# Two transformer blocks in one kernel: attention units weigh 2000 more in the sharing of expert rows beside the first half's block

## The chip, the cores and the metric

The kernel runs on one core of one Trainium2 chip. The metric is the device time of one execution in microseconds (us). Before the change the median of three runs is 4016.86 us (4007.53 to 4020.57).

## The reference, cut to what matters

512 tokens of width 1024, all in float32. A first block (RWKV and neighbourhood attention, not touched here) ends in a mixture of experts; a second block of two layers follows.

```python
# experts of the first block: 8 heads, 16 chosen rows of two tables per token and head
act = jax.nn.gelu(jnp.einsum('chkd,cd->chk', u_tab[i_c], x_c))
out = jnp.einsum('chk,chkd->cd', g_c * act, v_tab[i_c])

# second block, layer 0 (even mixer) and layer 1 (odd mixer: dilated attention)
for layer in range(2):
    x = x + mixers[layer](rms_norm(x, mix_norms[layer]))
    x = x + memory_cross_attention(rms_norm(x, xn), rms_norm(mem, mn), wq, wkv, wo)
    x = x + swiglu(rms_norm(x, fn), wg, wu, wd)      # hidden width 2816
return rms_norm(x, final_norm)
```

All attention of the second block is causal, so the first 256 tokens never need the last 256.

## The kernel before

The 512 tokens are four tiles of 128. Tiles 0 and 1 are the first half (h=0), tiles 2 and 3 the second half (h=1). For each tile, head and choice j (16 of them) POOL gathers two rows per token out of the tables by an indirect DMA (L2353, 128 rows of 4 KB, 0.52 MB): a u row, of which DVE takes the dot product with the token (`peer_dve`, L2483: a custom instruction and a read of its accumulator), and a v row, which DVE multiplies by the gated factor and adds to the tile's sum (L2469; for the first tiles TensorE does most of that). After the 16 dots of a head ACT takes their gelu (L2451) and DVE multiplies by the gates (L2491). The ring of buffers for gathered rows holds 8 of them in this phase.

While tiles 2 and 3 go through their experts (2 tiles x 8 heads x 16 choices = 256 steps, here called **slots**: one v row added, one u dot taken; the last 16 slots have a v row only), the whole second block for the first half of the tokens, called the block, is computed beside them: `second_pe`, `second_act` and `second_dve` with h=0. Afterwards the same code runs for h=1 with nothing beside it.

The three programs are generators that yield a number, a cost in made-up units, after each piece of work. `Beside` (L2357) shares them out: with the sum of all costs divided by 256, each slot lets the block go on until the costs it passed have used up the slot's part. DVE's program calls it twice a slot, once after the v row and once after the u dot. So the costs decide where in DVE's one instruction queue the rows of the experts stand between the instructions of the block:

```python
block = Beside(second(k, p, 0), k.second_cost, 16 * KN)     # L2391
...
def advance(self, part=1.0):                                 # L2363
    self.owed += self.each * part
    while self.owed > 0:
        x = next(self.steps, None)
        ...
        self.owed -= x
```

The block's stages are, in order: the experts' result and norms, `inputs_*` (7 products), 32 attention **units** of layer 0 (`units_pe`, `units_act`, `units_dve`; 16 of the sliding window, 16 latent), the output product, the cross attention's product and 8 units, its output product, the feed-forward (`ffn_*`, eleven rounds of gate, up and down products, each with 1 MB of weights), and the same again for layer 1 with 32 dilated units. The weights of each product come through four buffers of 1 MB (`load_wide`, L2780) and each is issued on SP's queue when the product before it in its buffer has ended. TensorE's products all stand in one helper (L2806, and L3684 for down).

A unit is one tile and one head: TensorE's scores (L3121), DVE's minimum with the mask (L3230, or L3234 for the cross attention), ACT's exp (L3191 or L3195), TensorE's transposes (L3153), ACT's copy (L3203), TensorE's output (L3162), DVE's division (L3252, L3257), and for every second one a transpose and a copy into the output (L3168, L3206). `unit_order` (L3053) pipelines them: while unit u is scored, unit u-1 is put out. Beside the units of layer 0 and of the dilated attention stand pieces of further products (`Fill`), one or two of which are taken per unit. Each unit ends in `yield unit_cost(x)`, where x.m is its number of keys (128 or 256 for h=0); the pieces of a product yield 427 for each of its matmul steps (`MM`).

Of the kernel before, what the change touches and what calls it, by code (L numbers as in the profile page):

```python
# [3094 lines left out]


def unit_cost(unit):
    return unit.m * 5 + 300


def both_halves(units, u):
# [25 lines left out]
def units_pe(k, p, a, name, units, fill, rate):  # L3127
    S, filled, made = k.S, 0, set()
    for step, u in unit_order(units):
# [6 lines left out]
        elif step == "rest":  # L3136
            yield from fill.rest()
        elif step == "pause":
            yield unit_cost(x)
        elif step == "scores":  # L3140
            yield from fill.until(x.mark, u - 1)
# [29 lines left out]
def units_act(k, p, a, name, units, fill, rate):  # L3171
    S = k.S
    for step, u in unit_order(units):
# [3 lines left out]
        if step == "fill":  # L3177
            yield from fill.take(rate, min(u + 1, len(units) - 1))
        elif step == "rest":
            yield from fill.rest()  # L3180
        elif step == "pause":
            yield unit_cost(x)
        elif step == "scores":
            yield from fill.until(x.mark, u - 1)
            s, bank = a.S[u % 2], k.bank[2 + u % 2]
            if x.nb < x.m and u >= 2:
                p.wait_ge(S.weights_filled, (name, u - 2))
            p.wait_ge(S.scores_low, key)
            if x.nb:
                last = x.nb == x.m and x.sink is None  # L3190
                p.e.activation(s[:, 0:x.nb], s[:, 0:x.nb], ACT.Exp, bias=low, scale=-1.0, accum_out=cols[:, 2:3]).then_inc(  # L3191
                    *(p.up(S.weights_exp, key) if last else p.up(S.scalar_step)))
            if x.nb < x.m:
                c = 3 if x.nb else 2
                p.e.activation(s[:, x.nb:x.m], bank[:, x.nb:x.m], ACT.Exp, bias=low, scale=-1.0,  # L3195
                               accum_out=cols[:, c:c + 1]).then_inc(*p.up(S.weights_exp, key))
            if x.sink is not None:
                p.e.activation(cols[:, 3:4], x.sink, ACT.Exp, bias=low, scale=-1.0).then_inc(*p.up(S.weights_exp, key))
        elif step == "weights" and weights_by(k, a, u) is S.act_weights:
            if u >= 2:  # L3200
                p.wait_ge(S.output_filled, (name, u - 2))
            p.wait_ge(S.weights_filled, key)
            p.e.activation(a.PT[u % 2][:, 0:x.m], k.bank[4][:, 0:x.m], ACT.Copy).then_inc(*p.up(S.act_weights, key))  # L3203
        elif step == "store" and stored_by(k, a, x.tile) is S.act_stored:
            p.wait_ge(S.store_filled, key)
            p.e.activation(x.dst, k.bank[4][:, 0:P], ACT.Copy).then_inc(*p.up(S.act_stored, key))  # L3206


def units_dve(k, p, a, name, units, fill, rate):
    S, stored = k.S, {}  # L3210
    for step, u in unit_order(units):
# [5 lines left out]
        elif step == "rest":  # L3217
            yield from fill.rest()
        elif step == "pause":
            yield unit_cost(x)  # L3220
        elif step == "scores":
            yield from fill.until(x.mark, u - 1)
# [935 lines left out]
```

## Time and profile before

| | |
|---|---|
| median of three runs | 4016.86 us (4007.53 to 4020.57) |
| profiled execution, its own time | 4020.22 us |
| its span, first to last instruction | 4018.4 us |
| TensorE busy | 3351.1 us (83%) |
| VectorE busy | 2197.6 us (55%) |
| ScalarE busy | 745.1 us (19%) |
| GpSimd busy | 1385.0 us (34%) |
| bytes moved | 834.04 MB |

The profile is of one execution. Busy shares are averages over stages with different limits, so they have to be read by stretches of the span. The phase in which the block stands beside the experts of tiles 2 and 3 goes from about 1815 to 2976 us.

### The profile page before, as it was taken

The page shows a single profiled execution, that of the slowest core. Times are in us where ns is not written, and L with a number is a line of the kernel's source. Part 1 is how long each engine was busy: PE and PEld are TensorE (multiplying, and loading weights), DVE is VectorE, ACT ScalarE, POOL GpSimd, SP SyncE. Part 2 cuts the span into 40 slices and gives each one's busy share as a digit, 9 for nine tenths or more (in the row PEclk, how much of TensorE's full clock was granted, in tenths as well). Part 3 has the DMA queues.
Part 4 walks back from the last instruction along what each step waited for, and adds up shares of the span by engine and source line. Part 5 has one row for each costly group of instructions (what it writes and reads, how often), then busy time and mean ns, then how long its engine had stood idle before and what let it go on. Part 6 is the DMA issues. An engine that isn't in the chain of part 4 may idle for free. (4 is left out here: it accounts for less than half of the span.)

```text
span 4018.4 us, 40100 instructions
## 1 busy us (share of the span) xinstructions
PE 3351.1 (83%) x14758; PEld 2479.8 (62%) x14758; DVE 2197.6 (55%) x4302; ACT 745.1 (19%) x1691; POOL 1385.0 (34%) x1219
## 2 busy tenths in 40 slices
PE   7778998888777787756677888778998999999999
PEld 3445647887333343424466776567876678877787
DVE  2434135455899989877677668877753320033201
ACT  2122122221211111111222002211012220022200
POOL 0641002221677767765344655545610000000000
PEclk9888889999888898988788999889999999999999
DMA  7230200003999999997578999879962134421343
GB/s 208 72 115 11 81 27 1 1 13 101 344 334 379 360 365 368 374 357 288 202 259 296 392 394 368 290 257 383 392 214 68 53 105 147 157 95 63 115 147 105
DMA packets 449223, 834.04 MB, mean 208 GB/s; under 512 B 46659, under 2 KB 291454, under 8 KB 449022
## 3 DMA queue, kind: packets, MB, share of 16 engines
q0 software_dynamic: 147456, 536.94, 35.9%
q1 hardware_dynamic: 301574, 294.56, 22.9%
q8 instruction: 118, 1.93, 0.2%
q14 instruction: 75, 0.61, 0.0%
HBM read 829.23 MB, written 2.17 MB: 207 GB/s over the span
## 5 line engine op out<-in xcount | busy, mean ns | idle before, releaser
L2806 PE MATMUL banks<-arena 128*128 128x256 f32 (+1 forms) x4992 | 1138.5, 387 | 80.5 <-DMA arena<-in_l_w_up 36.8
L2806 PEld LDWEIGHTS banks<-arena 128*128 128x128 f32 (+1 forms) x4992 | 961.8, 194 | 243.1 <-DMA arena<-in_l_w_up 40.8
L2353 POOL DMA_INDIRECT arena<-in_peer_u,arena x512 | 580.9, 1135 | 493.6 <-DVE arena L2483 185.1
L2353 POOL DMA_INDIRECT arena<-in_peer_v,arena x512 | 586.5, 1145 | 405.4 <-DVE arena L2469 244.4
L2483 DVE CUSTOM_DVE_ANT_0 arena<-arena 128x1024 f32<-128x1024 f32 x512 | 628.1, 1227 | 104.1 <-DMA arena<-in_peer_u,arena 80.0
L2425 PE MATMUL banks<-arena 128*128 128x512 f32 x768 | 415.6, 685 | 194.6 <-issue 68.4
L2469 DVE SCALAR_TENSOR_TENSOR arena<-arena 128x1024 f32<-128x1024 f32 x316 | 406.2, 1286 | 29.2 <-DMA arena<-in_peer_v,arena 15.1
L2425 PEld LDWEIGHTS banks<-arena 128*128 128x128 f32 x768 | 158.2, 218 | 408.4 <-issue 319.1
L3730 DVE TENSOR_TENSOR arena<-banks,arena 128x512 f32<-128x512 f32 x44 | 30.5, 692 | 514.9 <-PE banks L2806 514.8
L3684 PE MATMUL banks<-arena 128*128 128x256 f32 x1408 | 310.5, 378 | 0.0
L3684 PEld LDWEIGHTS banks<-arena 128*128 128x128 f32 x1408 | 265.7, 189 | 38.3
L842 PE MATMUL banks<-arena 128*128 128x512 f32 (+1 forms) x320 | 133.5, 567 | 39.0 <-DVE arena L986 18.2
L3705 ACT ACTIVATE arena<-banks 128x512 f32<-128x512 f32 x44 | 26.3, 598 | 687.0 <-PE banks L2806 629.8
L547 PE MATMUL banks<-arena 128*128 128x512 f32 (+1 forms) x336 | 131.4, 551 | 0.0
L1633 POOL TENSOR_TENSOR arena<-arena 128x512 f32<-128x512 f32 x48 | 52.5, 1093 | 222.3 <-DVE arena L1599 149.1
L2138 PE MATMUL banks<-arena 128*128 128x512 f32 (+1 forms) x320 | 123.5, 533 | 6.2 <-ACT arena L1911 3.5
L3230 DVE CUSTOM_DVE_ANT_0 arena<-banks,arena 128x256 f32<-128x256 f32 (+3 forms) x128 | 59.8, 467 | 122.5 <-PE banks L3121 115.7
L842 PEld LDWEIGHTS banks<-arena 128*128 128x128 f32 x320 | 65.5, 215 | 94.8 <-issue 68.6
L509 POOL TENSOR_TENSOR arena<-arena 128x2048 f32<-128x2048 f32 x16 | 57.3, 3603 | 193.1 <-ACTq L277 104.8
L3191 ACT ACTIVATE arena<-arena 128x256 f32<-128x256 f32 (+3 forms) x128 | 69.4, 542 | 293.1 <-DVE arena L3230 217.5
L3162 PE MATMUL banks<-arena 128*128 128x64 f32 (+1 forms) x720 | 119.0, 300 | 3.0 <-DVE arena L3257 3.0
L3153 PE MATMUL banks<-arena 128*128 128x128 f32 x360 | 80.4, 319 | 48.7 <-ACT arena L3206 32.8
(339 smaller groups left out, 4141.2 us busy)
## 6 DMA issues: line engine op xcount, KB each, us to landing
arena<-in_l_w_gate SPq DMA_DIRECT2D x44, 1024.0 KB
arena<-in_l_w_up SPq DMA_DIRECT2D x44, 1024.0 KB
arena<-in_l_w_down SPq DMA_DIRECT2D x44, 1024.0 KB
arena<-in_ada_w SPq DMA_DIRECT2D x24, 1024.0 KB, 8.6
arena<-in_l_w_qkv SPq DMA_DIRECT2D x24, 1024.0 KB
arena<-in_w_in SPq DMA_DIRECT2D x33, 512.0 KB
arena<-in_l_w_out SPq DMA_DIRECT2D x16, 1024.0 KB
arena<-in_peer_q_w SPq DMA_DIRECT2D x20, 512.0 KB
```

Of the source, the lines that this page charges most:

```text
L547: ins = p.e.matmul(k.bank[b][0:m, 0:n], k.W[slot][:, c, 0:m], rhs(c), start=c == 0, stop=c == c_n - 1, skip_group_check=True)
L842: ins = p.e.matmul(k.bank[b][0:m, 0:n], k.W[slot][:, c, 0:m], rhs(c), start=c == 0, stop=c == c_n - 1, skip_group_check=True)
L2138: ins = p.e.matmul(k.bank[4][:, cols], ws[j][:, c, :], k.HT[:, c, cols], start=c == 0, stop=c == DC - 1, skip_group_check=True)
L2353: p.e.indirect_dma_start(e.ring[slot], None, tables[table], bass.IndirectOffsetOnAxis(ap=e.IDX[h][:, t, j:j + 1], axis=0)).then_inc(*p.up( ...
L2425: ins = p.e.matmul(k.bank[b], e.diag[x % 4], e.ring[slot][:, half * T:half * T + T], start=h == 0 and j == 0, stop=h == HEADS - 1 and j == ...
L2469: p.e.scalar_tensor_tensor(out=e.ACC[t], in0=e.ring[slot], scalar=factor, in1=e.ACC[t], op0=ALU.mult, op1=ALU.add).then_inc(*p.up(S.rows_a ...
L2483: p.e.tensor_tensor_reduce(out=e.prod, in0=e.ring[slot], in1=e.H2[:, t, :], scale=1.0, scalar=0.0, op0=ALU.mult, op1=ALU.add, accum_out=e. ...
L2806: ins = p.e.matmul(out, left(c), right(c), start=c == 0, stop=c == c_n - 1, skip_group_check=True)
L3153: ins = p.e.transpose(k.bank[4][:, j * P:j * P + P], a.S[u % 2][:, j * P:j * P + P], k.ident)
L3162: ins = p.e.matmul(k.bank[5][:, 0:x.w], a.PT[u % 2][:, j * P:j * P + P], values, start=j == 0, stop=j == len(x.values) - 1, skip_group_che ...
L3191: p.e.activation(s[:, 0:x.nb], s[:, 0:x.nb], ACT.Exp, bias=low, scale=-1.0, accum_out=cols[:, 2:3]).then_inc(*(p.up(S.weights_exp, key) if ...
L3684: ins = p.e.matmul(k.bank[4 + o // 2][:, o % 2 * TH:o % 2 * TH + TH], w[:, r, P * o:P * o + P], a.hid[:, (i - 1) % 2, TH * r:TH * r + TH], ...
```

## The change

`unit_cost` returns 2000 more. Nothing else is edited:

```diff
 def unit_cost(unit):
-    return unit.m * 5 + 300
+    return unit.m * 5 + 2300
```

With h=0 there are 80 units, so the sum of the block's costs goes from 871,824 to 1,031,824 and the part of one of the 256 slots from 3405.6 to 4030.6. The costs that the code yields, added up by stage and divided by that part, give the slots that stand beside each stage:

| stage of the block, h=0 | units | cost before | slots before | slots after | difference |
|---|---|---|---|---|---|
| experts' result and 7 norms and scalings | 0 | 43,156 | 12.7 | 10.7 | -2.0 |
| inputs, 7 products | 0 | 47,234 | 13.9 | 11.7 | -2.2 |
| units of layer 0, while products stand beside them | 25 | 57,654 | 16.9 | 26.7 | +9.8 |
| units of layer 0, the last ones alone | 7 | 9,140 | 2.7 | 5.7 | +3.1 |
| products into and out of the cross attention, output products | 0 | 109,312 | 32.1 | 27.1 | -5.0 |
| cross units, two groups of 8 | 16 | 25,280 | 7.4 | 14.2 | +6.8 |
| feed-forward, two of 11 rounds | 0 | 450,912 | 132.4 | 111.9 | -20.5 |
| dilated units, while products stand beside them | 20 | 114,016 | 33.5 | 38.2 | +4.7 |
| dilated units, the last ones alone | 12 | 15,120 | 4.4 | 9.7 | +5.3 |

The instructions of TensorE, GpSimd and SP's queue keep their order. On VectorE rows change places with the block's instructions; on ScalarE the gelus do.

VectorE, among the last dilated units, before:

```order
L3257 TENSOR_SCALAR arena<-banks,arena 128x64
L2469 SCALAR_TENSOR_TENSOR arena<-arena 128x1024
L3230 ISA arena<-banks,arena 128x128
L3230 ISA arena 128x1
L3252 RECIPROCAL arena<-arena 128x1
L3257 TENSOR_SCALAR arena<-banks,arena 128x64
L3230 ISA arena<-banks,arena 128x256
L3230 ISA arena 128x1
L3252 RECIPROCAL arena<-arena 128x1
L3257 TENSOR_SCALAR arena<-banks,arena 128x64
```

The same place now:

```order
L3257 TENSOR_SCALAR arena<-banks,arena 128x64
L2483 ISA arena<-arena 128x1024
L2483 ISA arena 128x1
L2469 SCALAR_TENSOR_TENSOR arena<-arena 128x1024
L3230 ISA arena<-banks,arena 128x128
L3230 ISA arena 128x1
L3252 RECIPROCAL arena<-arena 128x1
L3257 TENSOR_SCALAR arena<-banks,arena 128x64
L2483 ISA arena<-arena 128x1024
L2483 ISA arena 128x1
L2469 SCALAR_TENSOR_TENSOR arena<-arena 128x1024
L3230 ISA arena<-banks,arena 128x256
```

Where one v row stood in two units, a u dot and a v row now stand in each.

VectorE in the feed-forward of layer 0, the start of one piece of the difference (L3730 closes a round of gate and up):

```order
+L2483 ISA arena<-arena 128x1024
+L2483 ISA arena 128x1
+L2469 SCALAR_TENSOR_TENSOR arena<-arena 128x1024
 L3730 TENSOR_TENSOR arena<-banks,arena 128x512
-L2469 SCALAR_TENSOR_TENSOR arena<-arena 128x1024
-L2483 ISA arena<-arena 128x1024
-L2483 ISA arena 128x1
-L2469 SCALAR_TENSOR_TENSOR arena<-arena 128x1024
```

Between two L3730 there are six slots in most rounds before and five in most rounds now.

ScalarE among the cross units of layer 0, one piece of the difference:

```order
 L3206 ACTIVATE arena<-banks 128x128
 L3203 ACTIVATE arena<-banks 128x256
+L2451 ACT_TABLE_LOAD
+L2451 ACTIVATE arena<-arena 128x16
+L3195 ACT_TABLE_LOAD
 L3195 ACTIVATE arena<-banks,arena 128x256
 L3206 ACTIVATE arena<-banks 128x128
```

A gelu with a table load before it and one behind it now stands between two units there.

## Rows read from the trace of the kernel before

**Rows 1.** The page: span, busy time of the engines, DMA share in 40 slices.

```profile
span 4018.4 us, 40100 instructions
PE 3351.1 (83%) x14758; PEld 2479.8 (62%) x14758; DVE 2197.6 (55%) x4302; ACT 745.1 (19%) x1691; POOL 1385.0 (34%) x1219
DMA  7230200003999999997578999879962134421343
```

**Rows 2.** Busy time by stretch: the two feed-forwards of the block.

```profile
core 0: us, PE busy (x) PEld busy (x) DVE busy (x) ACT busy (x) POOL busy (x), PEclk, DMA share, GB/s
2167.30:2429.60 262.30, 234.44 (x1041) 201.10 (x1042) 180.98 (x225) 17.72 (x23) 157.92 (x133) 0.97 1.02 386
2730.30:2975.90 245.60, 221.63 (x992) 190.13 (x991) 151.01 (x178) 17.72 (x23) 126.33 (x109) 0.97 0.98 366
```

**Rows 3.** Waits of PE and DVE, 2167.3 to 2429.6 us: total, times, longest.

```profile
PE banks L2806 <- DMA arena<-in_l_w_up: 18.8, 5, 5.1
PE banks L2806 <- DMA arena<-in_l_w_gate: 7.2, 3, 3.5
...
DVE arena L3730 <- PE banks L2806: 51.3, 11, 11.1
```

**Rows 4.** DMA in the same stretch: packets, MB, share of 16 engines.

```profile
DMA packets 43246, 101.21 MB, mean 386 GB/s; under 512 B 2575, under 2 KB 23899, under 8 KB 43233
...
q0 software_dynamic: 18582, 67.67, 66.4%
q1 hardware_dynamic: 24651, 33.37, 35.5%
```

**Rows 5.** By stretch: ten rounds, first to last L3730, twice with rows, once without.

```profile
2185.00:2419.80 234.80, 208.86 (x932) 178.94 (x931) 154.84 (x188) 15.62 (x20) 142.21 (x119) 0.97 1.04 394
2742.00:2973.90 231.90, 207.93 (x929) 178.17 (x928) 138.81 (x163) 15.62 (x20) 117.51 (x102) 0.97 0.99 370
3297.20:3498.10 200.90, 200.90 (x930) 175.38 (x929) 6.92 (x10) 5.98 (x10) 0.00 (x0) 1.00 0.47 152
```

**Rows 6.** By stretch: layer 0 units with products, alone; dilated units with products, alone.

```profile
1914.60:2036.00 121.40, 80.73 (x316) 52.76 (x314) 83.31 (x212) 39.49 (x128) 38.94 (x36) 0.76 0.60 200
2036.00:2051.60 15.60, 8.39 (x31) 6.26 (x30) 9.61 (x28) 4.65 (x18) 4.17 (x4) 0.61 0.67 212
...
2449.10:2589.00 139.90, 114.92 (x546) 91.43 (x544) 120.67 (x220) 35.20 (x100) 84.16 (x69) 0.95 0.96 346
2589.00:2615.10 26.10, 17.83 (x68) 12.74 (x69) 17.53 (x49) 7.92 (x30) 6.97 (x8) 0.50 0.53 157
```

**Rows 7.** By stretch: eight cross units for h=1 without rows, twice for h=0.

```profile
3240.20:3267.70 27.50, 18.73 (x104) 14.16 (x103) 10.18 (x32) 8.62 (x26) 0.00 (x0) 0.88 0.06 19
2110.30:2142.50 32.20, 17.52 (x69) 12.23 (x67) 17.54 (x36) 10.19 (x33) 8.04 (x10) 0.62 0.60 208
2669.40:2701.80 32.40, 17.46 (x69) 11.93 (x67) 17.57 (x36) 10.21 (x33) 7.88 (x9) 0.63 0.59 205
```

**Rows 8.** DVE's instructions in order: start, us; one slot with nothing between.

```profile
2298.24 1.28 DVE L2469 SCALAR_TENSOR_TENSOR arena<-arena 128x1024 f32<-128x1024 f32 x1
2299.55 1.23 DVE L2483 CUSTOM_DVE_ANT_0 arena<-arena 128x1024 f32<-128x1024 f32 x1
2300.71 0.08 DVE L2483 DVE_READ_ACCUMULATOR2_ANT arena<- 128x1 f32 x1
2300.82 1.28 DVE L2469 SCALAR_TENSOR_TENSOR arena<-arena 128x1024 f32<-128x1024 f32 x1
```

**Rows 9.** Gelus on ACT and the wait for them on DVE, 1815 to 2980 us.

```profile
L2451 ACT ACT_TABLE_LOAD  x15: 1283/1283/1283, 1901.2 to 2916.0; - x15
...
DVE arena L2491 <- ACT arena L2451: 17.2, 12, 8.3
```

**Rows 10.** By stretch: inputs; output product of layer 0; a norm and scaling.

```profile
1868.40:1914.60 46.20, 42.79 (x207) 36.34 (x206) 42.24 (x54) 5.50 (x10) 32.03 (x27) 1.00 0.93 346
2051.60:2080.20 28.60, 26.43 (x113) 22.71 (x114) 23.84 (x33) 2.54 (x8) 17.89 (x15) 0.86 0.83 287
2429.60:2449.10 19.50, 12.08 (x37) 9.14 (x36) 14.45 (x23) 5.79 (x8) 4.71 (x5) 0.65 1.00 367
```

## The prediction

> **What bounds the kernel now.** I read the page first, then the table of stretches, then the waits and the DMA view inside single stretches. The page [rows 1] says only that TensorE leads with 83% and that DMA is nearly full in the middle of the span, where the block stands beside the experts. The change acts in that phase alone, about 1815 to 2976 us, so the rest keeps its time.
>
> By stretch the phase falls into two kinds. In the feed-forwards the 16 DMA engines are full: share 1.02 and 0.98, at 386 and 366 GB/s [rows 2]. TensorE there waits for the weights of up and gate, 18.8 and 7.2 us in the first one, and DVE, which has little else to do, waits 51.3 us for TensorE [rows 3]. Two thirds of the DMA share are gathered rows, 67.7 MB of 101.2 [rows 4]. What this costs is read by comparing ten rounds beside rows with ten rounds of the same products in the second half with none beside them: 234.8 and 231.9 us against 200.9 [rows 5]. So the rows make the two feed-forwards about 34 and 31 us longer.
>
> In the units the reader sees the opposite. With the DMA share at 0.5 to 0.6 (0.96 only where the dilated products stand beside them), the limit is DVE's queue and the short chain TensorE, DVE, ACT, TensorE. DVE is busy 69% of the time in the units of layer 0, 86% in the dilated ones with products, 67% in the last dilated ones [rows 6] and 54% in the cross units [rows 7].
>
> **The change, part by part.** The cost table tells where slots go; the prices come from rows. One slot on DVE is 2.58 us: v row to v row, 2298.24 to 2300.82 [rows 8].
>
> 1. Feed-forwards, 10.3 slots fewer in each (66.2 to 55.9). In the first one the gathered 67.7 MB become 67.7 x 55.9 / 66.2 = 57.1, with 33.4 MB of weights 90.5 MB; at 386 GB/s that takes 234.6 us instead of 262.3, a gain of 27.7 [rows 2, 4]. TensorE's own floor is 262.3 - 33.9 = 228.4 [rows 2, 5]. DMA would still bind, by 6 us; two limits that close do not overlap perfectly, and I take 24. The second loses as many slots, its last 16 gather only one row each, and its cap is 31.0 [rows 5]; I take 23. Sum **-47**, bounds -36 and -65 (both caps reached).
>
> In the Trainium skill, the page "DMA: Bandwidth & Descriptors", section "Specifications", gives about 358 GB/s as the limit of HBM for one core. The 386 GB/s of [rows 2] lie above that, so here the measurement decides; by 358 the first feed-forward's gain would be an estimated 30 us and not 27.7.
>
> 2. Seven norms and scalings, inputs, output and cross products: 2.0, 2.2 and 5.0 slots fewer. In a norm's stretch DVE is busy 14.5 of 19.5 us and TensorE only 12.1, so DVE and its chain set the time [rows 10]: 2.0 x 2.58 = 5.2, taken as -5. In the inputs TensorE is busy 42.8 of 46.2 us, in the output product 26.4 of 28.6 [rows 10]: there a slot was nearly free, and taking it away gives -2 together. Sum **-7**, bounds 0 and -12.
>
> 3. Units of layer 0 with products, 9.8 slots more: DVE's 83.3 us busy become 83.3 + 9.8 x 2.58 = 108.6. As the slot's 2.6 us of DVE work fit into the time that the chain of the unit takes on ACT and TensorE, I expect waits to shrink until DVE is as full as in the dilated units with products, 120.7 / 139.9 = 86% [rows 6]: 108.6 / 0.863 = 125.8 against 121.4, **+4**. The last seven: (9.6 + 3.1 x 2.58) / 0.863 = 20.4 against 15.6, **+5**.
>
> 4. Dilated units with products, 4.7 slots more, where DVE and DMA are both full already: each slot at its full price, **+12**. The last twelve: (17.5 + 5.3 x 2.58) / 0.863 = 36.1 against 26.1, **+10**.
>
> 5. Cross units, 3.4 slots more in each group: (17.5 + 8.8) / 0.863 = 30.5, under the present 32.3, so they would hide. But the 3.7 slots now there cost 32.3 - 27.5 = 4.8 us, 1.3 each [rows 7]. Between 0 and 1.3 x 3.4 = 4.4 I take +1 each, **+2**.
>
> 6. ScalarE's gelus. Four of them (after slots 16, 64, 176 and 192) go from input, norm or feed-forward stretches to units, the others stay in their kind of stretch. Between exps each needs two table loads of 1.28 us, and DVE waits for them, now 17.2 us over 12 waits [rows 9]; among the units these loads stand in the chain. **+4** for the four less what their old places cost, bounds 0 and +8.
>
> TensorE's, POOL's and SP's orders are unchanged, so nothing is queued behind a new wait there. POOL waits for DVE to free ring buffers; a row that comes later on DVE is gathered later, and in the units the DMA share of 0.6 leaves room for it.
>
> The sum: -47 - 7 + 4 + 5 + 12 + 10 + 2 + 4 = **-17 us**, against the profiled execution's 4020.2 us: 4003. That execution is 3.4 us above the median of 4016.9, so in terms of the median the sum gives 4000; I say **4001**. Bounds: every moved slot absorbed in layer 0 and cross units (+0, with +22 for the dilated ones) and the caps reached give -65 - 12 + 22 = -55; all 29.7 slots at full price (+77) with the gelus at +8 and the small gains give -36 + 77 + 8 = +49.
>
> **The rivals.** A difference within 0.3%, 12 us, can't be told from no change for this kernel.
>
> *Absorbed.* The units of layer 0 and the cross units take their slots into waits wholly, and the feed-forwards come down to TensorE's floor: -60 - 7 + 22 + 4 = -41, so 3976. For it: DVE idles 38 us in the layer 0 units with products [rows 6] and only 25 us of work come. Against: the 1.3 us per slot in the cross units, where DVE is just as idle.
>
> *DVE saturated, the other side: slower.* A row is 1.2 to 1.3 us long and not divisible, and DVE takes its queue in order. If the v rows and u dots stand just before the minimum or the division that TensorE and ACT wait for, each moved slot costs its full 2.58 us, and the unit stages grow by 29.7 x 2.58 = 77. Against this the gains stay: -47 - 7 + 77 + 4 = +27, 4044. It decides from a mean of 1.7 us per moved slot (50 us of net gains over 29.7). For it: the last dilated units are a dense chain, and the dilated stage has no DVE time left. Against: 1.3 us in the only place where a price can be read [rows 7].
> A worsening goes with it. The granted clock is 0.95 in the dilated units with products, but 0.76 in those of layer 0, which have more gaps, and 0.50 in the last ones [rows 6]. If sparser products bring the dilated stage to 0.76, TensorE's 114.9 us become 114.9 x 0.95 / 0.76 = 144, above the stage's 139.9, and some 8 us come on top: 4052. The Trainium skill's "TensorE: Matmul & The Clock Gate", section "What's actually happening", states that the throttled clock is the default and activity releases it; by that rule thinner product stretches lose clock, and the rows at 0.76 and 0.50 agree with it.
>
> *Break-even.* The feed-forward gains are real but the units give them back at 1.3 to 2 us a slot: between -10 and +10, 4008 to 4028. That the change does nothing of what it says is excluded, as the order on DVE shows it.
>
> **How the numbers follow.** Forecast, between -30 and -5 us: 0.42. Absorbed or better, beyond -30: 0.13. Break-even, -5 to +10: 0.21. Saturated, above +10: 0.24, of which 0.05 with the lost clock. Over 12 us faster needs the sum at -12 or beyond: all of "absorbed" and 0.31 of the forecast, 0.44 together. Slower by over 12 us: 0.22 of the saturated case. The rest, 0.34, lies within. The range from **3974 to 4040** leaves out about one in ten on each side; it reaches to "absorbed" below and nearly to the saturated value above. Cases of both signs hold much of the chance; the likeliest one's own range is 3987 to 4012.
>
> **What would show it.** Right, step by step: ten rounds of feed-forward between first and last L3730 take 212 to 216 us, with TensorE's waits for up and gate under 10 us in the first (26.0 now); units of layer 0 take about 9 us longer in all, the dilated units about 22, cross groups stay within 2 us of 32; DVE's busy share in the units of layer 0 is near 86%; the second half's 1042 us from 2976 to the end do not move. Wrong: ten rounds over 225 us, which would mean DMA or the rows' order binds in another way; or unit stages longer by over 60 us in sum, with TensorE waiting for L3257 and L3230; or a granted clock near 0.8 in the dilated units with products.

## The result and the profile after

The changed kernel takes 4027.22 us (median of 19 runs, 4011.53 to 4037.50), the kernel before 4012.85 us (median of 19, 4000.91 to 4031.13). The ratio is 1.0032, with a 95% interval of 1.0020 to 1.0044: slower by about 13 us. I had forecast 4001 us, faster by 16; the measured time lies in the range, but on the other side of no change. The two profiled executions are no fair pair in their totals: that of before was 7 us above its median, that of after (4014.18 us) 13 us below. The parts of the span outside the changed phase differ by as much as the change does: behind the last L3730 of the first half come 1044.5 us before and 1030.5 after, and the eleven kernels of the experiments lie between these two whatever their weight. So I go by stages.

The busy time by stretch of the changed kernel, between the marks that answer to [rows 5], [rows 7] and [rows 6]: layer 0 units from first minimum to last division, cross units, ten rounds, dilated units, cross units, ten rounds.

```profile
core 0: us, PE busy (x) PEld busy (x) DVE busy (x) ACT busy (x) POOL busy (x), PEclk, DMA share, GB/s
1909.90:2077.90 168.00, 95.31 (x335) 62.36 (x335) 127.85 (x285) 46.19 (x149) 82.08 (x64) 0.65 0.71 236
2132.20:2171.40 39.20, 17.98 (x69) 12.68 (x67) 25.32 (x46) 12.96 (x36) 18.15 (x13) 0.60 0.64 213
2210.70:2418.60 207.90, 203.96 (x930) 176.23 (x929) 130.93 (x161) 14.32 (x19) 112.00 (x99) 0.99 1.04 392
2467.80:2642.50 174.70, 117.21 (x510) 90.21 (x508) 144.28 (x275) 40.84 (x128) 106.00 (x84) 0.79 0.91 316
2696.00:2735.00 39.00, 17.77 (x69) 12.50 (x67) 25.32 (x46) 12.93 (x36) 17.24 (x13) 0.60 0.63 212
2776.60:2981.90 205.30, 202.09 (x930) 174.94 (x929) 116.08 (x137) 14.32 (x19) 91.05 (x81) 1.00 0.97 364
```

And the same marks of the kernel before for the two unit stages that [rows 6] had cut in two (times in the texts and tables are taken from the exact starts and ends, so they can differ by 0.1 us from these rounded windows):

```profile
1919.00:2056.60 137.60, 87.83 (x335) 58.51 (x335) 94.98 (x245) 44.63 (x147) 41.56 (x39) 0.73 0.59 193
...
2472.10:2615.00 142.90, 109.73 (x509) 85.06 (x508) 116.41 (x241) 40.03 (x126) 75.52 (x63) 0.86 0.89 315
```

Side by side, in us, with the rest of the phase (norms, inputs, cross and output products and the ends of the feed-forwards) in one line. The slots of the cost table belong to whole stages; the column "counted" has the rows (L2469 and L2483) that the two traces show between these marks, two rows to a slot:

| stage | slots by cost | counted | before | after | difference | forecast |
|---|---|---|---|---|---|---|
| layer 0 units | +12.9 | +13 | 137.7 | 168.0 | +30.3 | +9 |
| cross units, both groups | +6.8 | +6 | 64.6 | 78.1 | +13.5 | +2 |
| dilated units | +10.0 | +11 | 142.9 | 174.7 | +31.8 | +22 |
| ten rounds of feed-forward, twice | -20.5 (eleven rounds) | -18.5 | 466.7 | 413.1 | -53.6 | -47 |
| the rest | -9.2 | -11.5 | 330.9 | 321.0 | -9.9 | -7 |
| all | 0 | 0 | | | +12.1 | -17 (with +4 for gelus) |

The waits in the first feed-forward show its limit gone: TensorE's waits for up and gate fall from 26.0 us [rows 3] to 3.9, and ten rounds stand 7 us from the 200.9 us without rows [rows 5].

```profile
PE banks L2806 <- DMA arena<-in_l_w_up: 3.4, 2, 2.5
PE banks L2806 <- DMA arena<-in_l_w_gate: 0.5, 1, 0.5
```

The units took the gain and more: 75.6 us for 30 counted slots, 2.5 us a slot on average, nearly VectorE's own 2.58 us of [rows 8]. The cross units tell why a stage in which VectorE is busy only 65% of the time hides nothing. One period of the changed kernel, in order of time (each `...` stands for lines left out):

```profile
2142.40 0.35 DVE L3257 TENSOR_SCALAR arena<-banks,arena 128x128 f32<-128x128 f32 x1 [2.27 <-PE banks L3162]
2142.78 1.23 DVE L2483 CUSTOM_DVE_ANT_0 arena<-arena 128x1024 f32<-128x1024 f32 x1
2142.93 0.42 PE L3168 MATMUL banks<-arena 128*128 128x128 f32 x1
...
2144.05 1.28 DVE L2469 SCALAR_TENSOR_TENSOR arena<-arena 128x1024 f32<-128x1024 f32 x1
...
2145.37 0.42 DVE L3234 TENSOR_REDUCE arena<-banks 128x1 f32<-128x256 f32 x1
2145.83 0.47 ACT L3195 ACTIVATE arena<-banks,arena 128x256 f32<-128x256 f32 x1 [3.91 <-DVE arena L3234]
...
2146.29 0.27 ACT L3206 ACTIVATE arena<-banks 128x128 f32<-128x128 f32 x1
...
2146.70 0.66 PE L3153 MATMUL banks<-arena 128*128 128x128 f32 x2 [3.35 <-ACT arena L3206]
2147.16 1.06 PE L3162 MATMUL banks<-arena 128*128 128x128 f32 x4
...
2148.36 0.35 DVE L3257 TENSOR_SCALAR arena<-banks,arena 128x128 f32<-128x128 f32 x1 [2.30 <-PE banks L3162]
```

It is a ring, a closed chain of waits (not the ring of buffers). The rows stand between a division and the next minimum. The minimum releases the exp; ScalarE's queue holds the copy L3206 of the block stored before behind that exp, though L3168, whose result it copies, had ended at 2143.35, nearly 3 us earlier; TensorE's transposes L3153 write into the bank that this copy reads, the output follows them, and the next division waits for the output. TensorE's waits of L3153 for that copy in this group (2132.2 to 2171.4 us) are

```profile
PE banks L3153 <- ACT arena L3206: 16.8, 6, 4.3
```

From division to division it takes 5.96 us, 2.97 of them from the one division to the next minimum, with a u dot and a v row in series. With one row there the trace of before has 4.70 us:

```profile
2123.19 0.35 DVE L3257 TENSOR_SCALAR arena<-banks,arena 128x128 f32<-128x128 f32 x1 [2.30 <-PE banks L3162]
2123.57 1.29 DVE L2469 SCALAR_TENSOR_TENSOR arena<-arena 128x1024 f32<-128x1024 f32 x1
...
2124.89 0.42 DVE L3234 TENSOR_REDUCE arena<-banks 128x1 f32<-128x256 f32 x1
...
2127.89 0.35 DVE L3257 TENSOR_SCALAR arena<-banks,arena 128x128 f32<-128x128 f32 x1 [2.30 <-PE banks L3162]
```

So the second row in a period costs 1.26 us, its whole length. Idle time of an engine inside such a ring is not room.

### The profile page after: what moved, and what is told of

It reads as the page before. It is cut to its first block and busy times, and to the rows that moved or that the text cites. A ratio compares the mean times of both kernels' runs of the same rounds, so it can differ in the third digit from the quotient of the medians.

```text
span 4012.4 us, 40100 instructions
## 1 busy us (share of the span) xinstructions
PE 3327.4 (83%) x14758; PEld 2464.1 (61%) x14758; DVE 2199.0 (55%) x4302; ACT 743.8 (19%) x1691; POOL 1393.6 (35%) x1219
## 3 DMA queue, kind: packets, MB, share of 16 engines
q0 software_dynamic: 147456, 536.94, 36.1%
## 5 line engine op out<-in xcount | busy, mean ns | idle before, releaser
L2483 DVE CUSTOM_DVE_ANT_0 arena<-arena 128x1024 f32<-128x1024 f32 x512 | 628.0, 1227 | 92.1 <-DMA arena<-in_peer_u,arena 73.0
L2425 PE MATMUL banks<-arena 128*128 128x512 f32 x768 | 406.0, 669 | 201.7 <-ACT arena L2444 131.4
L2469 DVE SCALAR_TENSOR_TENSOR arena<-arena 128x1024 f32<-128x1024 f32 x316 | 406.3, 1286 | 22.7 <-DMA arena<-in_peer_v,arena 12.0
L3730 DVE TENSOR_TENSOR arena<-banks,arena 128x512 f32<-128x512 f32 x44 | 30.5, 693 | 537.5 <-PE banks L2806 537.5
L842 PE MATMUL banks<-arena 128*128 128x512 f32 (+1 forms) x320 | 132.5, 564 | 40.2 <-DVE arena L986 19.4
L3153 PE MATMUL banks<-arena 128*128 128x128 f32 x360 | 79.8, 316 | 68.6 <-ACT arena L3206 48.3
L3168 PE MATMUL banks<-arena 128*128 128x128 f32 x96 | 35.7, 372 | 104.8 <-DVE arena L3257 70.3
```

Source lines behind the costliest of these rows:

```text
L842: ins = p.e.matmul(k.bank[b][0:m, 0:n], k.W[slot][:, c, 0:m], rhs(c), start=c == 0, stop=c == c_n - 1, skip_group_check=True)
L2425: ins = p.e.matmul(k.bank[b], e.diag[x % 4], e.ring[slot][:, half * T:half * T + T], start=h == 0 and j == 0, stop=h == HEADS - 1 and j == ...
L2469: p.e.scalar_tensor_tensor(out=e.ACC[t], in0=e.ring[slot], scalar=factor, in1=e.ACC[t], op0=ALU.mult, op1=ALU.add).then_inc(*p.up(S.rows_a ...
L2483: p.e.tensor_tensor_reduce(out=e.prod, in0=e.ring[slot], in1=e.H2[:, t, :], scale=1.0, scalar=0.0, op0=ALU.mult, op1=ALU.add, accum_out=e. ...
L3153: ins = p.e.transpose(k.bank[4][:, j * P:j * P + P], a.S[u % 2][:, j * P:j * P + P], k.ident)
```

## The experiments

**Where in the unit the rows stand.** e1 and e2 move the pause of a unit, with which its slots come, ahead of the division of the unit before; e1 at the weight of 2300, e2 at 300. The expectations of e1, e2 and e4 were written with wider marks, by which the cross groups of the changed kernel take 41.0 and 38.1 us and its dilated units 197 (166 before).

```diff
         yield "weights", u
+        yield "pause", u
         if u:
             yield "output", u - 1
             if units[u - 1].ends:
                 ended.append(u - 1)
-        yield "pause", u
```

> The changed kernel with the pause of a unit (the place where its slots stand) moved ahead of the division of the unit before, so that rows stand between the minimum L3234/L3230 and the division L3257 and no longer between the division and the next minimum. Number of slots beside each stage as in the changed kernel. Position theory (in the cross units a loop runs minimum, exp, copy of the stored block, transposes, output, division, 3.35 us, and the rows stand in series with it, 5.93 us with one slot): the rows now stand beside ACT and TensorE, a cross group falls from 41.0 and 38.1 us to 28 to 33, the units of layer 0 from 168 to 145 to 155, the dilated ones from 197 to 178 to 188, the whole to about 3975 us, 50 under the changed kernel. Saturation theory (VectorE has no time left for more rows): nothing changes beyond 5 us, 4022 to 4032. Clock theory (the units cost more because TensorE runs at the lower clock): as saturation, the stretches keep their length within 5 us.

> The kernel before (weight 300) with the same move of the pause. Position theory: the 29.7 slots fewer beside units gain less from the move, a cross group falls from 32.3 to about 28, layer 0 units from 137 to 125 to 132, dilated from 166 to 157 to 163, the whole to about 3988 us; the feed-forwards stay at 235 and 232 us for ten rounds, so this kernel ends above e1. Saturation and clock theories: as the kernel before within 5 us, 4008 to 4018.

| us | before | e2 | after | e1 |
|---|---|---|---|---|
| layer 0 units | 137.7 | 137.4 | 168.0 | 167.8 |
| cross units | 32.2, 32.4 | 27.8, 26.7 | 39.1, 39.0 | 34.7, 34.1 |
| dilated units | 142.9 | 158.9 | 174.7 | 203.3 |
| ratio to before (interval) | 1 | 1.0017 (0.9998 to 1.0036) | 1.0032 (1.0020 to 1.0044) | 1.0103 (1.0077 to 1.0129) |

In the cross units the ring theory holds: the same rows in another place cost 4 to 6 us less a group. For the whole it fails: e1's median is 34 us above the changed kernel's, where I had expected it 50 below. Layer 0 does not move, and the dilated units lose 16 and 29 us, since there TensorE waits for the division; in e1 (2475 to 2680 us) the first of its waits is

```profile
PE banks L3168 <- DVE arena L3257: 59.8, 15, 6.6
```

against 40.0 us in the changed kernel (2445.5 to 2642.6) and 22.8 us in the kernel before (2449.1 to 2615.1). So the cross and the dilated units have different steps that must not stand behind rows; for layer 0 these two runs show none.

**Taking the copy out of the ring.** e4 orders the store ahead of the next scores, in the first half; VectorE's order stays as it is. On ScalarE the copy L3206 now stands ahead of the exp, and on TensorE the store's transpose L3168 stands ahead of the scores L3121; no run has one of these without the other. e7 is the same at the weight of 300.

```diff
-        if u + 1 < n and not paired:
-            yield "scores", u + 1
-        for x in waiting:
-            yield "store", x
+        if first:
+            for x in waiting:
+                yield "store", x
+        if u + 1 < n and not paired:
+            yield "scores", u + 1
+        if not first:
+            for x in waiting:
+                yield "store", x
```

> The changed kernel with the store of a finished block ordered ahead of the next unit's scores (first half only), so that on ScalarE the copy L3206 no longer stands behind the next exp. VectorE's order is untouched, so the rows stay where they are. Position theory with ScalarE's queue as the link: the output of a unit no longer waits for the minimum behind the rows, a cross group falls from 41.0 and 38.1 us to 30 to 35, the 5 us of waits of L3153 for L3206 in a group nearly vanish; in layer 0 and dilated units, where every second unit stores, a part of that, 0 to 10 us each; the whole 10 to 30 us under the changed kernel. If the rows alone hold VectorE (saturation), cross groups keep 38 to 41 us.

> The kernel before (weight 300) with the store ahead of the next scores in the first half. If the gain of e4 (7 us in layer 0, 9 us in each cross group) is a matter of the chain alone: cross groups 32.3 to 28, layer 0 137.7 to 132, dilated unchanged, the whole 10 to 15 us under the kernel before, ratio 0.9965 to 0.9975. If it needs the many rows of weight 2300 to matter: ratio 0.999 to 1.001.

The busy time by stretch of the cross units of layer 0 in e4, and TensorE's wait for the stored block's copy there (e4's L3157 and L3210 are L3153 and L3206 of the changed kernel):

```profile
2140.10:2170.10 30.00, 17.51 (x69) 12.49 (x67) 25.29 (x46) 12.83 (x36) 18.13 (x13) 0.63 0.80 281
...
PE banks L3157 <- ACT arena L3210: 0.9, 2, 0.5
```

The same stretch of e7:

```profile
2101.90:2122.90 21.00, 11.96 (x69) 7.89 (x67) 17.54 (x36) 10.16 (x33) 7.58 (x9) 1.00 0.87 291
```

The wait that closed the ring falls from 16.8 to 0.9 us. The cross units fall to 30.0 and 30.5 us in e4 and to 21.0 and 21.7 in e7, layer 0 to 160.7 and 131.7, the dilated ones not at all (175.2 and 144.2). Ratio 0.9980 (0.9961 to 1.0000) for e4 and **0.9941 (0.9915 to 0.9967)** for e7, median 3988.59 beside 4010.46 us: this beats both kernels. e7 gained more than either case of its expectation. VectorE's busy time in a cross group is the 17.5 us of before, but now 84% of the stretch; e4 too has 84%. With the ring open, VectorE's queue is nearly full in both, and the 3 slots that the traces count more in e4 cost 9.0 us, 3.0 each. That is more than their 2.58 us; TensorE's granted clock differs too, 1.00 against 0.63, and these two parts are not separated.

**Half the work per row.** e5 and e6 let VectorE treat 512 of a row's 1024 elements for tiles 2 and 3, e5 at 2300, e6 at 300 (the other half of the v row and of the u dot is left out). Both, and e8 below, are single executions. A slot's busy time on VectorE falls from 2.58 us to 1.52, not quite to half (0.75 for the v row, 0.69 and 0.08 for the dot).

```diff
-p.e.scalar_tensor_tensor(out=e.ACC[t], in0=e.ring[slot], scalar=factor, in1=e.ACC[t], ...
+part = slice(0, T if t >= 2 else D)
+p.e.scalar_tensor_tensor(out=e.ACC[t][:, part], in0=e.ring[slot][:, part], scalar=factor, in1=e.ACC[t][:, part], ...
```

> The changed kernel, where for tiles 2 and 3 VectorE works on 512 of a row's 1024 elements only (gathers, their bytes and their order are whole; half of each v row and u dot is left out). A slot on VectorE falls from 2.58 to about 1.4 us. Theory that a moved slot costs VectorE's own time, whether its queue is full or its rows stand in series with the unit's chain: the units fall by about 1.15 us per slot, layer 0 from 168 to 140, dilated from 175 to 125 to 145 between first minimum and last division, cross groups from 39 to 31; together with e6 the surplus of the units over weight 300 falls from 76 to 30 to 45 us. Rival theories, clock, gelu tables or the DMA of the gathered rows: the surplus over e6 stays at 65 to 80 us. The ten rounds of feed-forward stay at 205 to 212.

> The kernel before with the same half rows (half of each v row and u dot left out for tiles 2 and 3). VectorE's time theory: layer 0 units from 138 to 122 to 130, dilated from 143 to 112 to 125, cross groups from 32.3 to 30; feed-forwards stay near 233 us for ten rounds, since DMA and not VectorE binds them. Rivals: all stretches as in the kernel before within 3 us.

| us | e6 (300) | e5 (2300) | surplus | surplus with whole rows |
|---|---|---|---|---|
| layer 0 units | 127.9 | 142.6 | 14.7 | 30.3 |
| cross units | 29.3, 29.6 | 33.1, 32.7 | 6.9 | 13.5 |
| dilated units | 130.3 | 144.8 | 14.5 | 31.8 |
| ten rounds, twice | 468.5 | 424.9 | -43.6 | -53.6 |

With less VectorE time per row the surplus of the units is 36.1 us instead of 75.6. That is inside the 30 to 45 expected; the gelus' tables and the gathered bytes are all there in e5, so a price that came from them would have stayed. For the clock it is not so in every stage. In a cross group e5 has 0.63, little above the 0.60 of the changed kernel, and the surplus halves all the same. In layer 0 and in the dilated units the change had lowered the granted clock and raised TensorE's busy time by 7.5 us each (87.8 to 95.3, 109.7 to 117.2), and in e5 that is gone too: 87.6 us and 110.0 us, as in e6. The dilated rows of e6 and e5:

```profile
2458.40:2588.70 130.30, 109.78 (x511) 85.27 (x510) 83.41 (x242) 40.17 (x126) 65.85 (x63) 0.86 0.94 344
2439.70:2584.60 144.90, 110.00 (x511) 85.28 (x511) 99.53 (x275) 40.88 (x128) 89.72 (x84) 0.85 1.01 381
```

So the runs show that VectorE's time per row brings the surplus about, but in those two stages not how much of it acts directly and how much by way of a lower clock.

**The gelus.** e8 replaces the gelu of tiles 2 and 3 by a copy at 2300, which needs no table.

```diff
-ACT.Gelu_apprx_tanh).then_inc(
+ACT.Gelu_apprx_tanh if t < 2 else ACT.Copy).then_inc(
```

> The changed kernel, where for tiles 2 and 3 the gelu on ScalarE is a plain copy (the gelu is left out), so no table is loaded for it. Theory that the gelus moved to the units are a large part of the 76 us: seven of them stand in units, and units fall by over 20 us. Theory that rows on VectorE are the price: units fall by 0 to 12 us in all, 1 to 2 us per gelu in a unit; feed-forward within 3 us.

Layer 0 units 168.5, cross 38.5 and 38.0, dilated 171.5 us: 4.3 us less than in the changed kernel in all, for the seven gelus that stand in units there (three did before). Their share is small, as the second theory has it.

**Which exchange loses.** e3 keeps the cross units at 300 in the changed kernel. e10 gives the feed-forwards the 55.9 slots of the changed kernel but leaves norms, inputs and products theirs. e11 is e10 with the store first.

```diff
-    return unit.m * 5 + 2300
+    return unit.m * 5 + (300 if unit.w == P else 2300)      # e3
```

```diff
-    return unit.m * 5 + 300
+    return unit.m * 5 + 1172                                # e10
...
+def lighter(steps):
+    for x in steps:
+        yield x * 69 // 82 if isinstance(x, int) else x
...
-        yield from ffn_pe(k, p, a, l)
+        yield from lighter(ffn_pe(k, p, a, l))
```

> The changed kernel, but the 16 cross units keep the weight of 300. Their slots go back from 7.1 to about 3.8 a group, those of each feed-forward up from 55.9 to 57.7. Position theory (a slot in a cross unit costs its full 2.58 us, one in a feed-forward that now runs at TensorE's floor costs next to nothing): cross groups back to 32 us, feed-forward within 3 us, the whole 12 to 17 us under the changed kernel. Rival (a slot costs the same wherever VectorE is given it): no more than 3 us of difference.

> The kernel before, where units cost 872 more and the pieces of the feed-forward 69/82 of their cost, so that the sum of the costs stays. A feed-forward has 55.8 slots as in the changed kernel (before 66.2), the units of layer 0, cross and dilated 27.9, 11.5 and 46.2 (before 19.6, 7.4, 37.9), all norms, inputs and output products keep theirs. Theory of two equal prices (a slot costs 2.6 us of DMA in a feed-forward and 2.58 us of VectorE in a unit, and the loss of the change is what it paid for the 9.2 slots that it took from norms and products): ten rounds at 205 to 212 us twice, units up by 20.4 x 2.55 = 52 us, the whole as the kernel before, ratio 0.998 to 1.002. Rival (the loss sits in the exchange between feed-forward and units itself): ratio 1.003 or above.

> e10 and the store ahead of the next scores. By the theory of equal prices it ends where e7 ended, ratio 0.992 to 0.997; if light feed-forwards help once the store is out of the way, below 0.991.

e3 was a miss: ratio 1.0053 (1.0031 to 1.0076). The cross units did fall, to 30.7 and 32.8 us, but the layer 0 units took +4.8, the dilated ones +4.6, and the ten rounds rose from 207.8 and 205.3 to 219.3 and 215.9 us. I had called a slot nearly free in a feed-forward that runs at TensorE's floor; 1.8 slots more brought rounds of 26 to 30 us back. Each of these is one profiled execution, and the seven kernels with 55.8 or 55.9 slots lie at 205 to 213, so the size of that step is known roughly only; in its two feed-forwards e3 stands 7 and 3 us above the highest of them.

e10 came out as the theory of two prices has it: the units +19.4, +9.7 and +24.0 us, 53.1 in all (expected 52), the ten rounds -48.2, ratio 1.0008 (0.9984 to 1.0033). The exchange between feed-forward and units is nearly a tie, 48.2 us against 53.1, for 19 counted slots given and 20 taken. By the ratios alone e10 can't be told from the changed kernel (1.0032), as the intervals overlap. e11 ended at 0.9930 (0.9908 to 0.9953), not to be told from e7.

**The opposite of the change.** e12 lets a unit cost 1.

```diff
-    return unit.m * 5 + 300
+    return 1
```

> The kernel before with a unit's cost of 1, the opposite of the change: cross units have no slot, layer 0 units 8.9 and dilated ones 29.7 (before 19.6 and 37.9), a feed-forward 75.3 (before 66.2), the rest 8.7 more in all. Equal prices down to the chain without rows: dilated 143 to 122 us, layer 0 137.7 to 112 to 118, cross 32.3 to 27 to 28 each, ten rounds up by 22 us each, norms and products up by 5 to 9: ratio 0.997 to 1.002. If instead rows in units had been hidden so far (my prediction's view): layer 0 and cross keep 130 or more and 30 or more, and the whole is 1.005 or above.

Ratio 1.0040 (1.0019 to 1.0061), a little outside what I expected. Its first rows (layer 0 and cross units):

```profile
1925.00:2039.70 114.70, 77.46 (x334) 53.16 (x332) 68.30 (x212) 41.00 (x142) 22.10 (x20) 0.78 0.44 150
2095.40:2121.90 26.50, 16.89 (x67) 11.92 (x67) 7.47 (x25) 8.79 (x31) 1.68 (x2) 0.62 0.34 133
```

The miss lies in the rest of the phase. Layer 0 and cross units came as expected, the dilated ones stopped at 135.5 us (122 expected), the ten rounds rose by 17 us each (22 expected), but norms, inputs and products took 21.6 us more where I had expected 5 to 9: 11 slots more at 2.0 us each, while the 11.5 that the change took away there gave 0.9 each. Without rows a cross unit's period is 3.81 us (divisions at 2105.21 and 2109.02), so the first row in it costs 0.9 us and the second 1.26. The first is partly hidden: in e12 the minimum waits 0.47 us for TensorE's scores.

The kernels together give the price of a slot by stage, each line in the order e12, before, e10, after. The slots are those counted in the traces between the marks, and each time is of one execution:

| stage | slots | us | us per added slot |
|---|---|---|---|
| layer 0 units | 9, 19.5, 28, 32.5 | 114.7, 137.7, 157.1, 168.0 | 2.2, 2.3, 2.4 |
| dilated units | 22, 31, 39, 42 | 135.5, 142.9, 166.9, 174.7 | 0.8, 3.0, 2.6 |
| cross units, a group | 0, 4, 5.8, 7 | 27.0, 32.3, 37.1, 39.1 | 1.3, 2.8, 1.5 |
| ten rounds, mean of two | 63.3, 55.3, 45.8, 46 | 250.5, 233.3, 209.3, 206.6 | 2.1, 2.5 |

The weight of 300 stands at the bend of the dilated stage: below it a slot is cheap there, above it a slot costs VectorE's 2.58 us or somewhat more.

## Why the prediction was wrong

**What was right.** The feed-forwards: DMA bound, given back nearly to TensorE's floor, -53.6 us against -47 and inside the bounds. The changed kernel's 413.1 us are the lowest of six kernels with the same slots and whole rows (the others 418.6 to 419.9), and 466.7 to 468.5 is the span of four with the slots of before, so the typical gain is about 50. Norms and products, -9.9 against -7. The gelus' +4 for the four moved ones was not measured by itself; all seven in units together are worth 4.3 us. Both signs that I had named for being wrong came: the unit stages grew by over 60 us in sum, with TensorE's waits for L3257 in the dilated stage going from 22.8 to 40.0 us, and the granted clock there fell to 0.79. The saturated rival had the units' price right: 77 us predicted for it, 75.6 measured, and with the rest it had said +27 where +12 to +14 came. I gave it 0.24. That 4027 us lies within 3974 to 4040 is owed to the width of the range, not to the sum.

**Which step failed.** Steps 3 to 5 of the sum, where I filled VectorE up to 86% in every kind of unit and let the waits take the slots. In layer 0 this gave +9 for 12.9 slots and +30.3 came, with VectorE at 76% and not 86%; in the cross units +2, and +13.5 came. The sentence that failed is that the slot's 2.6 us "fit into the time that the chain of the unit takes on ACT and TensorE". What the runs showed in its place, for the cross units: the rows stand in series with that chain. The period above shows it, e1 and e2 show that moving the rows inside the unit changes the time with the number of slots kept, e4 and e7 that storing first does, and e5 and e6 that the surplus follows VectorE's time per row. For layer 0 the price of 2.2 to 2.4 us a slot is measured and the surplus halves with half rows, but which of its steps are in series was not taken apart and stays open: moving the pause did nothing there, and the store gave 6 to 7 us.

**The 1.3 us that misled.** I priced a cross slot from [rows 7] as the difference to the same units in the second half. These have a granted clock of 0.88 and share copies with VectorE, so they need not equal the first half without rows; as it happened they do, e12's groups taking 26.5 and 27.5 us against 27.5. And 1.3 us is the mean price of the first four slots (table above). But it is not the price of the next: from 4 to 7 slots a group took 6.8 us more, 2.3 each. The trace of before had that in it, since in its period of 4.70 us the row already stands between the division and the minimum that ScalarE waits for.

**A size.** In the dilated units I forecast +22 and +31.8 came, nearly all of the miss in the units with products beside them, step 4's +12. Cut behind the twentieth division, the stage before and the first part after are

```profile
2472.10:2582.80 110.70, 89.55 (x430) 70.73 (x429) 93.95 (x180) 30.17 (x89) 65.95 (x53) 0.95 0.97 349
2582.80:2615.00 32.20, 20.17 (x79) 14.33 (x79) 22.45 (x61) 9.86 (x37) 9.57 (x11) 0.54 0.62 198
...
2467.80:2599.40 131.60, 97.40 (x431) 75.94 (x429) 107.78 (x197) 29.55 (x89) 79.09 (x64) 0.88 0.94 334
```

The units with products took 20.9 us more for 5.5 counted slots, of which VectorE's time explains 14. TensorE's busy time there rose by nearly 8 us as its granted clock fell from 0.95 to 0.88: a part of the lost clock that one rival named, though no run separates what it costs. The last twelve units took 10.9 us more, where +10 was forecast, but that agreement is partly luck: the 26.1 us that I had read for them [rows 6] held only ten divisions, the right stretch is the 32.2 us above. The changed kernel's last twelve show the queue full:

```profile
2599.40:2642.60 43.20, 19.84 (x80) 14.30 (x81) 36.56 (x79) 11.29 (x39) 27.01 (x21) 0.52 0.80 264
```

36.6 us of 43.2 are busy and the waits of VectorE there sum to about 3 us, the rest being gaps between its instructions: here 85% busy is a full queue. The phase also began at 1831 us, not at the 1815 that I wrote; no term hung on that.

**The sum, seen again.** By the counted slots, one costs 2.5 to 2.9 us in the ten rounds, where DMA binds (e10: 48.2 us for 19; the change: 53.6 for 18.5), and 2.5 to 2.7 us in the units (75.6 for 30; e10: 53.1 for 20). So the 18.5 slots that went from the one to the other were near a tie. The change's loss is in the other 11.5, taken from norms, inputs, products and the ends of the feed-forwards at a gain of 9.9 us and paid for at 2.5 each, 29 us.

## What to carry to other kernels

Before work is moved beside a stage because an engine idles in it, follow one period of that stage in order of time and see whether the inserted work stands between a release and its wait. If it does, its full length is the price, whatever the busy share, from the point on where nothing else there ends later (here the first row of a cross unit cost 0.9 us and the second 1.26). Price both ends of an exchange in the same unit: here a row cost the same in DMA time where it left as in VectorE time where it arrived, so the exchange could not pay, and what was taken elsewhere, where a slot was cheap, decided the sign. When a queue in the ring holds a ready instruction behind one that waits, as ScalarE held the copy behind the exp, look at that order first: storing first gave 0.9941, and none of the redistributions tried here was faster than the kernel before.

## What the runs showed that was not expected

With the store first at weight 300, TensorE ran a whole cross group at a granted clock of 1.00 (2.4 GHz), where the kernel before had 0.62, a mixture of both levels: its busy time fell from 17.5 to 12.0 us for the same instructions, and the group from 32.2 to 21.0 us, although what had been removed were waits of 2 us at a time. In its second group the clock is 0.93 (21.7 us). So a part of e7's gain is the clock's, and its size is not separated. The first group begins at the full clock in the kernel before too: 1.00 from 2110.3 to 2114.0 us, then 0.57 to its end. The Trainium skill's "TensorE: Matmul & The Clock Gate", section "What's actually happening", says that activity releases the throttle. The runs go with that in so far as the shorter a group is, the higher its clock tends to be (e2's 26.7 us at 0.73, e4's 30.0 at 0.63); but e12's group of 26.5 us, with no row and no wait for L3206 above 1.2 us, has 0.62, so what let e7 keep the clock stays open. In the second half's groups, with no rows at all, it stands at 0.88 [rows 7].

Delays of the feed-forward fall on few rounds. Apart from the first, most rounds take about 21 us and the others up to 31; in the first feed-forward the changed kernel has 25.9 and 22.3 us, and e3, with 2 counted slots more, 26.4, 23.6 and 30.1. Its ten rounds are 11 us longer than the changed kernel's, twice.
